# Sixteen more hops of a delta rule between projection tiles, sixteen fewer beside attention, in a hand-woven Trainium2 kernel

## The reference

```
def trunk_layer(x, ...):                       # twice, DEPTH = 2
    h = rms_norm(x, norm1_g) * (1 + scale1) + shift1
    u = h @ w_in                               # one input projection, split into the parts below
    gdn = gdn_mixer(...)                       # gated delta rule, 4 heads, chunks of 64 tokens
    att = dsa_attend(...)                      # index scores -> top-k of keys -> softmax attention
    ssm = ssd_mixer(...)                       # Mamba-2 SSD, 8 heads
    x = x + gate1 * (concat(gdn, att, ssm) @ w_out)
    h2 = rms_norm(x, norm2_g) * (1 + scale2) + shift2
    y = (silu(dwconv(h2 @ w_gate)) * (h2 @ w_up)) @ w_down
    return x + gate2 * y

def _gdn_chunk(S, (q, k, v, g, beta)):         # per chunk and head; S is carried from chunk to chunk
    a = strict_lower((k*beta) k^T * decay)     # 64 x 64
    u, w = solve(I + a, [v*beta, k*beta*exp(g)])
    v_new = u - w S
    o = (q*exp(g)) S + tril(q k^T * decay) v_new
    S = S*exp(g_last) + (k*exp(g_last - g))^T v_new
```

## Time and profile before

| | |
|---|---|
| median of 3 runs | 4767.0 us |
| the profiled execution | 4766.97 us |
| its span, first to last instruction | 4765.2 us |
| PE busy, share of span | 4351.0 us, 91% |
| DVE busy | 1670.4 us, 35% |
| ACT busy | 989.7 us, 21% |
| mean granted TensorE clock | 0.956 of full speed |

### The profile page before, as it was taken

The page is one execution under the profiler, slowest core; times in us unless marked ns, Lnnn a source line. Parts: engine busy times, 40 slices in busy tenths (PEclk is TensorE's granted clock), DMA queues, the critical chain, the costliest instruction groups (busy, mean ns, idle before and its releaser), DMA issues.

```text
span 4765.2 us, 54789 instructions
## 1 busy us (share of the span) xinstructions
PE 4351.0 (91%) x22086; PEld 2401.9 (50%) x22086; DVE 1670.4 (35%) x4123; ACT 989.7 (21%) x2045; POOL 67.2 (1%) x125
## 2 busy tenths in 40 slices
PE   4999888888989999999979998879897999999996
PEld 2545444557545555555535454445654555555553
DVE  2246776646122222100022667774532111111001
ACT  1124454234010000000012344434420000000001
POOL 0000000000000000000000000000000000000000
PEclk8999999899989999999989999879998999999998
DMA  4124111222012221111022121112311111111111
GB/s 178 39 103 145 43 43 42 96 90 102 28 59 80 102 85 60 34 32 37 25 88 59 47 66 43 49 69 94 127 33 38 36 32 36 36 32 34 35 35 44
DMA packets 111293, 292.42 MB, mean 61 GB/s; under 512 B 9280, under 2 KB 57088, under 8 KB 104640
## 3 DMA queue, kind: packets, MB, share of 16 engines
q1 hardware_dynamic: 100816, 243.62, 15.4%
q0 software_dynamic: 9936, 40.58, 2.2%
q10 hardware_dynamic: 288, 4.72, 0.2%
HBM read 243.59 MB, written 45.03 MB: 61 GB/s over the span
## 4 chain that ended last, share of the span: by engine, by line
PE 71%; DVE 11%; issue 10%; DVEq 3%; ACT 3%; PEld 1%; ACTq 1%; SPq 0%; DMA 0%; PEldq 0%; POOL 0%; POOLq 0%
PE PS L746 31%; PE PS L766 12%; PE PS L1283 7%; PE PS L1245 5%; DVE big L1674 2%; DVE big L1671 2%; DVE hT L1674 2%; DVE big L1809 1%; PE PS L869 1%; PE PS L1181 1%; PE PS L702 1%; PE PS L808 1%; PE PS L1196 1%; PE PS L1201 1%; PEld PS L730 1%
## 5 line engine op out<-in xcount | busy, mean ns | idle before, releaser
L746 PE MATMUL PS<-hT,ring 128*128 128x512 f32 (+1 forms) x4512 | 1476.6, 490 | 95.5 <-DVEq L1720 89.5
L746 PEld LDWEIGHTS PS<-hT,ring 128*128 128x128 f32 x4512 | 746.6, 192 | 823.6 <-issue 733.4
L766 PE MATMUL PS<-hT,ring 128*128 128x512 f32 (+1 forms) x2304 | 866.0, 522 | 0.0
L1283 PE MATMUL PS<-big,ring 128*128 128x512 f32 (+1 forms) x2112 | 683.4, 487 | 3.0 <-DVE big L1674 3.0
L766 PEld LDWEIGHTS PS<-hT,ring 128*128 128x128 f32 x2304 | 379.0, 199 | 326.9 <-issue 314.3
L1283 PEld LDWEIGHTS PS<-big,ring 128*128 128x128 f32 x2112 | 346.4, 191 | 340.0 <-issue 336.6
L1671 DVE SCALAR_TENSOR_TENSOR xT<-PS,mod,xT 128x1024 f32<-128x1024 f32 x32 | 41.1, 1284 | 871.0 <-PE PS L1283 657.6
L1674 DVE TENSOR_TENSOR big<-big,PS 128x512 f32<-128x512 f32 (+2 forms) x200 | 154.4, 795 | 519.4 <-PE PS L746 449.5
L1632 ACT ACTIVATE fext<-PS 128x1024 f32<-128x1024 f32 x44 | 45.1, 1024 | 1119.6 <-PE PS L746 1119.6
L2346 DVE TENSOR_SCALAR big<-fext,par 128x1024 f32<-128x1024 f32 x44 | 35.8, 814 | 656.2 <-ACTq L1634 656.2
L1328 ACT ACTIVATE big<-xT 128x1152 f32<-128x1152 f32 x40 | 46.0, 1161 | 1056.6 <-DVEq L2311 625.0
(11 more groups left out here) (340 smaller groups left out, 3565.6 us busy)
## 6 DMA issues: line engine op xcount, KB each, us to landing
big<-in_w_ada SPq DMA_DIRECT2D x72, 512.0 KB, 5.4
ring<-in_w_in SPq DMA_DIRECT2D x54, 512.0 KB, 3.5
scr<-big POOLq DMA_DIRECT2D x40, 576.0 KB, 3.1
ring<-in_w_gate SPq DMA_DIRECT2D x44, 512.0 KB, 3.6
ring<-in_w_up SPq DMA_DIRECT2D x44, 512.0 KB, 3.6
hT<-in_kcache SPq DMA_DIRECT2D x16, 1024.0 KB, 7.0
hT<-in_vcache SPq DMA_DIRECT2D x16, 1024.0 KB, 7.1
ring<-in_w_down SPq DMA_DIRECT2D x32, 448.0 KB, 3.3
```

The costliest lines, as they stand in the source:

```text
L746: i = mm(pset(n % 2)[:, c0:c0 + m], w[:, k, :], hT[:, k, c0:c0 + m], start=(k == 0), stop=(k == KT - 1))
L766: x = mm(PS[:, o:o + m], w[:, k, :], hT[:, k, c0:c0 + m], start=(k == 0), stop=(k == KT - 1))
L1283: i = mm(pset(m % 2)[:, c0:c0 + n], w[:, k - k0, :], act[:, k * TOK + c0:k * TOK + c0 + n], start=(k == 0), stop=(k == NF - 1))
```

## The change

The number of G hops in the first of the two weaves goes from 96 to 112; the rest, now 16 instead of 32, stay beside attention. 96 is three pairs and the first 12 hops of pair 3; 112 is exactly four pairs. Nothing is added or taken away: the same instructions run with the same operands, in another order on each engine, in both layers. Because `weave` spreads evenly, every G hop of the first stretch comes a little earlier relative to the projection, and in the second the sample tile's hops start at once and stand further apart.

```
         D_A = 12 * DH
         D_I = D_A - DH - I_HOPS
         B_A = 27
-        G_D = 96
+        G_D = 112
         order = weave(D=DH) + weave(D=I_HOPS, I=I_HOPS) + weave(D=D_I, A=A_HOPS, B=B_A) + \
             weave(D=D_HOPS - D_A, G=G_D, B=B_HOPS - B_A) + weave(G=G_HOPS - G_D, T=T_HOPS) + weave(S=S_HOPS)
```

## The result

The kernel after takes 4841.73 us (median of 4 runs, 4835.67 to 4842.06) against 4766.47 us beside it: ratio 1.0155, 95% interval 1.0137 to 1.0173, 75 us slower. The forecast was 4784 us with a range to 4808. The direction was right, the time lies outside the range.

A forecast was written before the change was run, and what follows sets the result against it. The prediction took the rule's chain PE, DVE, ACT to pace much of the first weave and exponentials to hold many attention steps. Cost 26 less gain 17.5 gave 8.5 us a layer, 17 in two: 4767 to 4784 us, range 4758 to 4808.

The forecast's parts named there:

- Where the end is set: First weave: neither PE nor DVE is full; the rule's chain PE, DVE, ACT sets much of the pace, not projection products.
- The price of the hops: First weave: 16 added hops cost 22.8 us ahead of the closing hops plus 3 beside them, 26 a layer (13.5 to 37).
- a pair's period: First weave: the time per pair, about 122 us before, should become 112 to 116 us.
- The waits: First weave: L957's waits for ACT become 8 instead of 6; the closing part stays at 68 to 74 us.
- SP and POOL at nothing: Sample state load at attention's start and earlier output writes on these two engines' queues: claimed to cost nothing.
- The gain in attention: Attention: losing 16 hops shortens it by 17.5 us a layer, between 10 and 24.
- Steps 0 to 16: Attention's first half: slack and DVE delays give 9.1 us, sample hops take back about 1, leaving 8 us.
- Steps 17 to 31: Attention's second half: 7 hops fewer remain, gaining 6 us; the narrow products L1000 only move from step 30 to 25.
- The end: End of attention: z, its DVE step and idle time leave the way to SSD's first product, gaining 3.5 us.
- Attention hardly gains: Attention: exponential loop and lower clock hold it; gain 10, cost 30, 20 us slower a layer, 4807 us; chance 0.16.
- Absorbed: First weave: hops fill idle time, costing 13.5 us against 18 gained; 4.5 us faster a layer, 4758 us; chance 0.16.
- an even trade: Both stretches: about 1.1 us a hop, cost and gain both 17 to 18 us, time stays 4767 us; chance 0.20.

The follow-up runs named there:

- e2: Against the kernel before: 96 hops woven as before, the next 16 run alone, then the sample hops beside attention; 4851.98 us, ratio 1.0178.
- e5: Kernel before (96 hops) with every counting operation of the top-k search working on 8 elements instead of a whole row; 4712.7 us, ratio 0.9885.
- e7: Kernel before (96 hops) with half of the 512-column products left out of the last 12 projection tiles; 4757.69 us, ratio 0.9977.
- e1: Kernel after (112 hops), but the first 18 attention hops run alone and the 16 sample hops lie between the other 18; 4828.2 us, ratio 1.0128.
- e4: Kernel before with 84 instead of 96 hops in the first weave, leaving 44 beside attention; 4808.41 us, ratio 1.0086.
- e17: Kernel after (112 hops) with every search hop of the first weave one search slot earlier; 4847.69 us, ratio 1.0166.
- e14: Kernel before, still 96 hops, with 10 moved from ahead of the search's closing hops to among them; 4785.85 us, ratio 1.0041.
- e10: Kernel before (96 hops) with the turn of a pair's first tile and its gate one hop later, in the z hop; 4754.5 us, ratio 0.9969.
- e16: The kernel of e10 run once more, on this chip beside the others; 4751.99 us, ratio 0.9967.

## Why the prediction was wrong, by its own steps

- **Where the end is set: right, but not followed through.** "The rule's chain PE, DVE, ACT sets much of the pace, not the products" fits e2, e5 and e7. If it holds, the products beside a hop cost little, and their whole time must not be taken off.
- **The price of the hops, a failed step.** I took windows of 63.7, 68.9 and 64.5 us around the same 16 hops, took 36.8 to 40.4 us of projection products off and called what is left, 27.1, the price. e7 shows that of 79 us of such products 6 to 8 lie on the path, at most some 26. The difference was thus no price, only a number between the ends. By steps: for 13 hops ahead of the closing part 22.8 us were forecast, 35.4 measured in both layers; for the closing part 3, measured 0.6 / 2.0; together 26 against 36.0 / 37.4. PE's work was right (13.5, measured 13.7); the idle time that comes with the hops was forecast at 12.5 (26 - 13.5) and is 23.8. My upper end, 37, contained the one and just missed the other.
- **What had been at hand.** The same text forecast a pair's period of 112 to 116 us. The measured ones are 110.8, 120.5, 111.3 and 117.1, mean 114.9 (116.2 in layer 1), so that was nearly right; and four of them are the 460 us of the stretch. My sum had 447, which fits only the lowest end of that period, four times 112. The middle of my own range would have given 456, and I didn't hold the two against each other.
- **The waits.** L957 waits 8 times, as forecast; the closing part went from 68.3 to 70.5 us, within 68 to 74. The 10 table loads in place of 8 were counted right; what the two more cost, 1.28 us of ACT each in the trace, no run isolates.
- **SP and POOL at nothing: not contradicted.** Nothing of theirs is among PE's or DVE's long waits.
- **The gain in attention, the larger failure.** 17.5 us were forecast, 1.3 and 4.1 came (2.8 and 5.3 by the first logits): 14.8 a layer too much in the mean, where the price of the hops was 10.7 too low. Steps 0 to 16: forecast 8, measured -0.5 (layer 1: 2.9); I overrated the slack (9.1, in e1 at most 6.4) and underrated the sample hops, which are spaced out and yet take 6.9 (3.4) back, in step 3 by DVE's queue as above. All durations in that sum were those of the trace before, and the granted clock of these steps fell from 0.95 to 0.87. Steps 17 to 31: forecast 6, measured 0.6 (0.9). I had written that the 128 narrow products L1000 "only move from step 30 to step 25". There they cost more: the interval of maxima that holds them went from 8.3 to 14.7 us, while the one that lost them went from 9.8 to 4.8. The end: forecast 3.5, measured 1.2 (22.4 to 21.2; layer 1: 0.2). The lines are from the kernel after; the same L1000 products took 4.09 us before.

```profile
1047.37 4.66 PE L1000 MATMUL PS<-xT,big 64*64 64x16 f32 x128
1051.96 0.61 PE L1146 MATMUL PS<-xT,cb 128*128 128x512 bf16 x1
1052.50 3.68 PE L1150 MATMUL PS<-hT,big 128*64 128x512 f32 x8
```

- **The rivals.** "Attention hardly gains", 0.16, had the right mechanism on its side of the sum: the loop holds the pace (76.2 us with no hop at all), and the first steps' granted clock fell. Its gain of 10 was still far too much, and its cost of 30 too small. "Absorbed" and "an even trade" are excluded: the price would have had to be 1.1 us a hop or less, and is 2.3.
- **The sum.** Cost 36.7 less gain 2.7 is 34 us a layer (mean of both), 68 in two. 3.8 us ahead of the stretch vary from run to run (its start lies between 452.9 and 456.7 us in all kernels). Behind layer 1's stretch it is 4.7 us more, between the layers 1.4 less. It doesn't go with the 112 hops: e1, with 112, has nothing more there, and e4, with 84, has 4.4. It lies in the first 100 us, ahead of the output projection L1245, where the granted clock is 0.93 in the kernels that have it (after, e4, e17) and 0.95 in those that haven't (before, e1, e14); what tips it is open. 68 + 3.8 + 4.7 - 1.4 = 75.1.

Shown by the runs: 16 hops more in the first weave cost about as much as they take alone, 36.0 and 37.4 us against 41 and 45 at the lower clock, and attention gives next to nothing for losing them. Neither the search's counting nor the wait for the normalisation nor the wait at L1482 is the cause by itself, and PE's projection products are for the most part not on the path. That the price is the round trips between the engines is what is left after these, and fits e2; no run shortens the round trips themselves. To the first maximum, 84, 96 and 112 hops lie on one line, 398.4, 425.8 and 461.8 us, 2.3 us a hop in either step (layer 1: 398.3, 429.4, 466.8, 2.6 and 2.3), but these are three of the five values run. Open: what lifts 92 by 13 to 19 us and 104 by 6 us above that line and moves 112 by 7 us with the phase. That the hops of the jobs happen to meet better or worse fits it; which meeting it is, no run isolates. Because attention hides no more than 32 hops and every hop ahead of it has a price, 96 is the best of the five values run.

The best version that the experiments point to is e10's: 96 as before, the turn one hop later, 4754.5 and 4752.0 us (e10 and e16), 0.3% faster than before.

## What to carry to other kernels

When several jobs are interleaved hop by hop on in-order queues, price a hop by its bare round trip (run the hops with nothing beside them, and look at the clock that they were granted there), not by what is left of a window after another job's work is taken off; subtract only what an experiment shows to be on the path. An experiment that leaves out work on PE can lower PE's clock: read the granted clock and the busy time of what is left before saying what the work was worth. Price what a stretch gives back with the same care as what it costs: here that was the larger error. Two engines at half load are no room for more hops of a chain: idle time that belongs to the chain's exchanges comes again with each hop added. Before a forecast goes out, work it out a second way, from the rate of the whole stretch, and trust neither until they agree; and where one wait grows, look whether shortening it shortens the stretch before calling it the cause.

## What the runs showed that I had not expected

- Leaving out 65 us of products in 353 lowered PE's granted clock from 0.93 to 0.80. With 112 hops the kernel was no faster for the smaller work, while PE's other products were busy some 28 us longer: to the first maximum 470.2 against 461.8 us in layer 0, 465.7 against 466.8 in layer 1.
- Attention takes the same time with 16 as with 32 hops of the rule beside it (rest 189.8 and 191.1 us), 205.5 with 36 and 239.1 with 44.
- Sixteen hops among the search's closing operations take 49 us, behind them 41 to 45: to interleave cost more than to append.
